# Seven of eight products of a residual norm on GpSimd instead of VectorE, in a float32 two-block kernel

## What is computed

```python
for i in range(DEPTH_2):
    y = rmsnorm(h, pre_norm[i])
    if i % N_MIXERS == 0:
        y = attention_mixer(y, ...)
    else:
        y = gla_mixer(y, ...)
    h = h + rmsnorm(y, post_norm[i])
```

## Time and profile before

| | |
|---|---|
| median of 3 runs | 2413.5 us (2413.14 to 2414.39) |
| profiled execution, its own time | 2413.42 us |
| its span | 2411.6 us |
| TensorE busy | 2392.1 us, 99% |
| VectorE busy | 1633.2 us, 68% |
| ScalarE busy | 1160.0 us, 48% |
| GpSimd busy | 88.3 us, 4% |
| HBM read | 409.86 MB, 171 GB/s |

### The profile page before, as it was taken

How to read it: one execution, slowest core, us unless ns; L and a number is a source line. 1 busy time by engine, 2 the same in 40 slices (tenths; PEclk the granted TensorE clock), 3 DMA queues, 4 the chain that set the end, 5 groups by cost and what they waited for, 6 DMA issues and landing times.

```text
span 2411.6 us, 40899 instructions
## 1 busy us (share of the span) xinstructions
PE 2392.1 (99%) x15928; PEld 2196.9 (91%) x15928; DVE 1633.2 (68%) x2630; ACT 1160.0 (48%) x1663; POOL 88.3 (4%) x114
## 2 busy tenths in 40 slices
PE   9999999999999999999999999999999999999998
PEld 7889999999988888888888889999999989999987
DVE  7777867756666766567656776666666567766765
ACT  6554545434445444334443346555555354555543
POOL 0000100000010000000000002000000100000000
PEclk9999999999999999999999999999999999999999
DMA  7556875566666666666666667655565645645553
GB/s 286 169 175 175 256 197 126 140 161 187 181 188 186 187 189 194 188 186 186 187 194 188 188 176 205 172 150 161 147 162 130 165 113 157 173 133 150 158 158 105
DMA packets 752433, 417.64 MB, mean 173 GB/s; under 512 B 44408, under 2 KB 740736, under 8 KB 752256
## 3 DMA queue, kind: packets, MB, share of 16 engines
q1 hardware_dynamic: 749760, 412.89, 60.9%
q10 hardware_dynamic: 2496, 2.27, 0.3%
HBM read 409.86 MB, written 2.11 MB: 171 GB/s over the span
## 4 chain that ended last, share of the span: by engine, by line
PE 95%; DVE 3%; ACT 1%; issue 0%; DMA 0%; DVEq 0%; ACTq 0%; SPq 0%
PE ps_unit L258 33%; PE ps_unit L260 17%; PE ps_unit L263 12%; PE ps_unit L265 11%; PE ps_unit L264 11%; DVE w_lo L241 1%; PE ps_score L1113 1%; ACT w_hi L234 1%; PE ps_score L693 0%; PE ps_score L692 0%; PE ps_score L638 0%; PE ps_score L637 0%; PE ps_score L910 0%; PE ps_out L931 0%; PE ps_norm L931 0%
## 5 line engine op out<-in xcount | busy, mean ns | idle before, releaser
L241 DVE TENSOR_TENSOR w_lo<-raw,w_hi 128x1024 fp32r<-128x1024 f32 (+1 forms) x746 | 874.5, 1211 | 217.1 <-ACT w_hi L234 216.3
L234 ACT ACTIVATE w_hi<-raw 128x1024 fp32r<-128x1024 f32 (+1 forms) x766 | 777.1, 1042 | 440.5 <-PE ps_unit L260 221.5
L258 PE MATMUL ps_unit<-a_hl,w_hi 128*128 128x512 f32 x1812 | 636.2, 394 | 1.4 <-DVE g_buf L1364 0.7
L258 PE MATMUL ps_unit<-b_hl,w_hi 128*128 128x512 f32 x1792 | 629.5, 394 | 0.6 <-DVE w_lo L241 0.6
L260 PE MATMUL ps_unit<-a_hl,w_lo 128*128 128x256 f32 x1812 | 508.2, 280 | 0.0
L260 PE MATMUL ps_unit<-b_hl,w_lo 128*128 128x256 f32 x1792 | 502.6, 280 | 0.0
L258 PEld LDWEIGHTS ps_unit<-a_hl,w_hi 128*128 128x128 f32 x1812 | 340.2, 188 | 78.4 <-DVE w_lo L241 1.2
L258 PEld LDWEIGHTS ps_unit<-b_hl,w_hi 128*128 128x128 f32 x1792 | 336.4, 188 | 77.1 <-DVE w_lo L241 1.0
L263 PE MATMUL ps_unit<-b_hl,w_hi 128*128 128x272 f32 (+1 forms) x1376 | 398.9, 290 | 0.7 <-DVE w_lo L241 0.7
L265 PE MATMUL ps_unit<-b_hl,w_lo 128*128 128x272 f32 (+1 forms) x1376 | 395.9, 288 | 0.0
L264 PE MATMUL ps_unit<-b_hl,w_hi 128*128 128x272 f32 (+1 forms) x1376 | 395.0, 287 | 0.0
(11 more groups left out here) (432 smaller groups left out, 2104.8 us busy)
## 6 DMA issues: line engine op xcount, KB each, us to landing
raw<-in_attn_w_in SPq DMA_DIRECT2D x96, 512.0 KB, 4.9
raw<-in_gla_w_in SPq DMA_DIRECT2D x96, 512.0 KB, 4.6
raw<-in_w_in SPq DMA_DIRECT2D x88, 512.0 KB, 4.8
raw<-in_w_ffn_gate SPq DMA_DIRECT2D x88, 512.0 KB, 4.6
raw<-in_w_ffn_up SPq DMA_DIRECT2D x88, 512.0 KB, 4.7
raw<-in_w_fox SPq DMA_DIRECT2D x64, 512.0 KB, 4.3
raw<-in_w_ffn_down SPq DMA_DIRECT2D x64, 512.0 KB, 4.6
raw<-in_w_out SPq DMA_DIRECT2D x32, 512.0 KB, 4.5
```

Of the source, the lines that this page charges most:

```text
L234: act.activation(hi[:, b % 4, 0:size], raw[:, b % 8, 0:size], ACT.Copy)\
L241: dve.tensor_tensor(lo[:, b % 4, 0:size], raw[:, b % 8, 0:size], hi[:, b % 4, 0:size], ALU.subtract).then_inc(lo_ready, 1)
L258: pe.matmul(dst.rearrange("p (a n) -> p a n", a=2), wh, x2[:, :, k0 + k, 0:T], start=start and k == 0, stop=False)
```

## The change

GpSimd gets the products of the pairs 1 to 7: it waits for all gains (`y_gain`) and for the factors (`s_rs`), runs seven 128x544 multiplications one behind another and signals each (`ys_p`). VectorE keeps the two small products of pair 0; for the other pairs it waits for GpSimd's product and only adds. GpSimd's two memsets stand behind the products now. Nothing that is computed changes.

```diff
-        xs_sq = sem("x_new_sq")
+        xs_sq, ys_p = sem("x_new_sq"), sem("y_scaled_pool")
...
                     n = k.stop - k.start
-                    dve.tensor_tensor(y[:, k, :], y[:, k, :], rms3[:, 0:n], ALU.mult).then_inc(ys, n)
-                    dve.wait_ge(ys, k.stop)
+                    if m == 0:
+                        dve.tensor_tensor(y[:, k, :], y[:, k, :], rms3[:, 0:n], ALU.mult).then_inc(ys, n)
+                        dve.wait_ge(ys, k.stop)
+                    else:
+                        dve.wait_ge(ys_p, m)
                     dve.tensor_tensor(X[:, k, :], X[:, k, :], y[:, k, :], ALU.add).then_inc(yr, n)
...
                     pool_square(pool, 51 + 4 * i + s, (s + 1) % 2, TM)
+            pool.wait_ge(y_gain, KC)
+            pool.wait_ge(s_rs, 8)
+            for m in range(1, KC // 2):
+                k = slice(2 * m, 2 * m + 2)
+                pool.tensor_tensor(y[:, k, :], y[:, k, :], RS[:, :].unsqueeze(1).broadcast_to([P, 2, TM]),
+                                   ALU.mult).then_inc(ys_p, 1)
             pool.wait_ge(s_nrm, 4)
             pool.memset(lgk_all[0], 0.0)
```

## The result

| | before | changed |
|---|---|---|
| median of 10 runs | 2414.26 us | 2420.44 us |
| all runs | 2413.14 to 2414.76 | 2419.71 to 2421.37 |
| profiled execution, its own time | 2413.42 us | 2421.37 us |
| its span | 2411.6 us | 2419.5 us |
| TensorE busy | 2392.1 us | 2394.9 us |

The ratio is 1.0026 with a 95% interval of 1.0017 to 1.0036: slower by 6.2 us, more than the 0.2% that a measurement tells from no change. Ratios further down leave out two executions that took several times as long as all others, 8383.03 us of the kernel with memsets and 13498.13 us of one with another order. VectorE lost seven products and is busy for longer than before.

The account below looks back on a forecast made before the run. VectorE was taken to bound the stretch until chunk 6, TensorE from there and the kernel overall. Turns cost 7.6, leaving chunk 2 6.0 late; less 0.8 gives 5.2, and 2413.42 + 5.2 = 2418.6 us, range 2414.8 to 2420.9.

Parts of the forecast that it names:

- What bounds the stretch: From VectorE's first product with token factors: VectorE bounds until chunk 6, TensorE from there; at most 2.5 us winnable.
- The loss per product: VectorE loses 1.12 us to each GpSimd product of 1.35, since one engine reads while the other stands.
- Both bounds: Limits on VectorE's loss to one GpSimd product: nothing, or all of its 1.35 us.
- Seven turns, 7.6: GpSimd's seven products go in between VectorE's early instructions, two costing 1.0 together, the other five 1.12 each: 7.6 us.
- The stretch longer by 5.2 at full clock: Chunk 2 starts 6.0 us late, vanished later waits give back 0.8; the stretch ends 5.2 later, at 1979.9.
- The clock: TensorE's granted clock stays full through 4.5 us of idling ahead of chunk 0; its fall was left to a rival.
- strict turns at full clock: Main case: VectorE and GpSimd alternate over reading and TensorE's clock stays full; 2418.6 us, chance 0.47.
- rival 1: Strict turns, and TensorE's clock falls in the gaps ahead of chunks 0 to 2: 1.7 us more, 2420.3; chance 0.19.
- The price of 1.7: Cost in us of a fallen TensorE clock, from fourteen dummy products started over 4.5 at program start and 2.8 here.
- The predicted time: Whole kernel: profiled execution of before, 2413.42 us, plus 5.2 gives 2418.6.
- Rival 2, VectorE keeps its turn: GpSimd enters only where VectorE pauses; together 1.8 us more, 2415.3, within 0.2%; chance 0.22.
- The rule on reading: A VectorE instruction with two SBUF inputs and a GpSimd instruction reading SBUF exclude each other for the whole instruction.

Follow-up runs that it names:

- the kernel with memsets: Changed kernel with GpSimd's seven products replaced by memsets of the same pieces of y, products of pairs 1 to 7 left out: median 2411.63 us, ratio 0.9989.
- another order: Kernel before, all products on VectorE, the rests of pair m - 1 between product and addition of pair m, weight rest one pair later: median 2414.86 us, ratio 1.0003.
- the dummy products: Changed kernel with 18 more dummy products of TensorE in the gaps ahead of chunks 0, 1 and 2: median 2418.79 us, ratio 1.0019, stretch 30.0 us.
- two other kernels with first gaps of 3.3 and 3.4: Kernel before without its seven dummy products of TensorE (3.3), stretch 26.1 us; changed kernel with only pairs 1 to 3 on GpSimd (3.4), stretch 26.6 us.
- the first four experiments: Not numbered; the text's first four headings: changed kernel with dummy products, 2418.79 us; with GpSimd memsets, 2411.63 us; with GpSimd reading one input; with fewer GpSimd products.

## Why the prediction was right, and where not

- **What bounds the stretch**: right. Only the waits up to chunk 6 could be won, 2.5 by my sum, and the kernel with memsets, where VectorE lost nothing, won 2.5.
- **The loss per product**, 1.12 from the rows at 228 and 1494: it measured 1.02 to 1.15. Both bounds, nothing and the whole 1.35, are excluded.
- **Seven turns, 7.6**: measured 7.6. Chunk 0 was to start at 1956.3; less the 0.94 it started at 1956.3. Chunk 2: 1961.7 forecast, 1961.8 measured.
- **The stretch longer by 5.2 at full clock**: 5.1 with the dummy products.
- **The clock**: the step that failed. I gave strict turns at full clock 0.47 and rival 1 only 0.19, because the clock had stayed full for 5 us of idling at the end, and 4.5 is less. All 10 runs of the changed kernel have a mean granted clock of 0.997 or 0.998, and it fell in two other kernels with first gaps of 3.3 and 3.4, and once behind gaps of 0.92 and 0.95. The tail was one sample, read as if the length of a gap decided. The price of 1.7, from the two rows of dummy products, measured 1.8, which is in part luck: the slow spell was 10.3 long, and only its last 4.0, from chunk 2's start at 1962.70 on, found TensorE without waits; half of 4.0 is the estimate that this trace gives. The Trainium skill, TensorE: Matmul & The Clock Gate, "Why this matters for your kernels", warned that idle gaps bring the clock down; that held here, and the trace agrees with the 0.50 over 10.3 us.
- **The predicted time**, 2418.6, is 1.8 short. In the stretch that is the clock. Between the medians it is not all of it: the change cost 6.2 where 5.2 was forecast, 1.0 more, and the other 0.8 is that the median of before over 10 runs is 2414.26 and not the 2413.4 that the forecast started from. So it is chance that rival 1's 2420.3 lies so near the median of 2420.44: its difference of 6.9 was 0.7 too much and its start 0.8 too low. The range, 2414.8 to 2420.9, holds the result, and the sign was right.
- **Rival 2, VectorE keeps its turn**: wrong here, for copies as well.
- **The rule on reading** from the Trainium skill, SBUF — State Buffer, "Who interferes with whom": the traces agree that a VectorE instruction with two inputs meets a GpSimd instruction that reads (two inputs cost 1.1, one 0.3 to 0.4) and not one that only writes (a memset cost nothing). They do not agree that one shuts out the other for its whole instruction: VectorE lost 1.1 to a product of 1.35, and 0.3 to 0.4 both to a copy of 0.84 and to a multiplication of 1.86. VectorE instructions with one input were not tried.

The medians differ by 6.2, the stretches by 6.9. The profiled execution of before is among its quick ones, 0.8 under the median, and that of the changed kernel is its slowest, 0.9 over; how much of the 0.7 this makes was not tried.

## What to carry to other kernels

Before work goes to a second engine, look in the trace for a place where both already run instructions of that kind, and take the price from what the *other* engine's instruction lost there, not from the length of the one moved. Here each product saved VectorE 0.8 and cost it 1.1. And where a delay opens a gap on TensorE, count the clock as part of the price: gaps of 0.9 kept it in one execution and lost it in another, so one gap that did no harm is no licence.

## What the runs showed that was not expected

- A GpSimd multiplication by a constant is 1.86 us long for 544 columns and holds VectorE up no longer than a copy of 0.84 does, 0.32 to 0.44.
- The clock can fall behind gaps of 0.9: it did in the profiled execution with the weight rest behind pair 4, while that of before, with the same gaps, kept it. Whether it also makes the spread of before's runs stays open. Of the 19 that were measured beside the first four experiments, those with a mean granted clock of 1.000 took 2413.03 and 2413.82, and those with 0.998 between 2414.11 and 2416.41. But among those measured beside later ones a run with 0.998 took 2413.84 and one with 1.000 took 2414.54.
- VectorE's slack behind chunk 6 is small: 0.6 us of waiting taken from chunk 6 came back as 0.4 at chunk 10.
